# Summing the modulation's partial products: 32x32 blocks turned and added on VectorE, quarters added in column tiles on TensorE

## What is computed

```python
cond = jax.nn.silu(c)                       # (1, 2048)
mod = cond @ w_ada[l] + b_ada[l]            # (1, 6144)
shift, scale, gate = jnp.split(mod, 3, axis=-1)
h = rms_norm(x, norm_g[l]) * (1.0 + scale[:, None, :]) + shift[:, None, :]
...
x = x + gate[:, None, :] * y
```

## Time and profile before

| | |
|---|---|
| median of three runs | 2553.03 us (2550.57 to 2553.16) |
| the profiled execution, its time | 2552.88 us |
| the profiled execution, its span | 2551.6 us |
| TensorE busy | 2510.9 us, 98% of the span |
| VectorE busy | 1644.1 us, 64% |
| ScalarE busy | 842.1 us, 33% |
| GpSimd busy | 392.3 us, 15% |

### The profile page before, as it was taken

The page is one execution under the profiler, slowest core; times in us unless marked ns, Lnnn a source line. Parts: engine busy times, 40 slices in busy tenths (PEclk is TensorE's granted clock), DMA queues, the critical chain, the costliest instruction groups (busy, mean ns, idle before and its releaser), DMA issues.

```text
span 2551.6 us, 30016 instructions
## 1 busy us (share of the span) xinstructions
PE 2510.9 (98%) x11928; PEld 2175.2 (85%) x11928; DVE 1644.1 (64%) x2187; ACT 842.1 (33%) x1139; POOL 392.3 (15%) x295
## 2 busy tenths in 40 slices
PE   8989999999999999999999999989999999999997
PEld 7878888888888888888888888878888888888886
DVE  6788889888988776545455775557565563244434
ACT  5222222222222322233322333332566564333321
POOL 0035344353443421000000000020000000000001
PEclk9999999999999999999999999989999999999998
DMA  5333333333333433667666675533322222322333
GB/s 184 106 99 128 115 114 105 124 117 109 125 109 126 141 122 130 221 215 255 196 204 204 217 240 202 200 102 132 100 87 77 85 88 87 116 99 93 122 124 116
DMA packets 119867, 353.07 MB, mean 138 GB/s; under 512 B 15408, under 2 KB 22832, under 8 KB 119728
## 3 DMA queue, kind: packets, MB, share of 16 engines
q1 hardware_dynamic: 119728, 351.16, 41.4%
HBM read 321.68 MB, written 23.07 MB: 135 GB/s over the span
## 4 chain that ended last, share of the span: by engine, by line
PE 95%; DVE 2%; issue 1%; POOL 0%; ACT 0%; DMA 0%; SPq 0%; DVEq 0%; POOLq 0%; ACTq 0%
PE bank L524 28%; PE bank L525 28%; PE bank L526 28%; PE bank L691 2%; PE bank L692 2%; PE bank L693 2%; PE bank L734 1%; PE bank L724 1%; PE bank L589 1%; PE bank L577 1%; DVE X L1836 0%; DVE SO L1434 0%; PE bank L715 0%; PE bank L717 0%; PE bank L514 0%
## 5 line engine op out<-in xcount | busy, mean ns | idle before, releaser
L1153 DVE TENSOR_TENSOR WL<-W,WH 128x1024 fp32r<-128x1024 f32 (+1 forms) x456 | 602.4, 1324 | 464.5 <-ACT WH L829 463.9
L829 ACT ACTIVATE WH<-W 128x1024 fp32r<-128x1024 f32 (+1 forms) x456 | 478.2, 1051 | 940.4 <-PE bank L526 706.7
L524 PE MATMUL bank<-hH,WH 128*128 128x512 f32 x1792 | 682.7, 381 | 12.7 <-DVE WL L1153 8.6
L525 PE MATMUL bank<-hL,WH 128*128 128x512 f32 x1792 | 680.9, 380 | 0.0
L526 PE MATMUL bank<-hH,WL 128*128 128x512 f32 x1792 | 680.6, 380 | 0.0
L524 PEld LDWEIGHTS bank<-hH,WH 128*128 128x128 f32 x1792 | 339.6, 189 | 69.7 <-DVE WL L1153 9.0
L526 PEld LDWEIGHTS bank<-hH,WL 128*128 128x128 f32 x1792 | 339.7, 190 | 48.5
L525 PEld LDWEIGHTS bank<-hL,WH 128*128 128x128 f32 x1792 | 339.7, 190 | 47.9
L524 PE MATMUL bank<-h2H,WH 128*128 128x512 f32 x640 | 245.5, 384 | 0.1
L525 PE MATMUL bank<-h2L,WH 128*128 128x512 f32 x640 | 242.6, 379 | 0.0
L526 PE MATMUL bank<-h2H,WL 128*128 128x512 f32 x640 | 242.6, 379 | 0.0
(11 more groups left out here) (260 smaller groups left out, 3585.4 us busy)
## 6 DMA issues: line engine op xcount, KB each, us to landing
W<-in_w SPq DMA_DIRECT2D x335, 512.0 KB, 3.7
W<-in_ada SPq DMA_DIRECT2D x96, 512.0 KB, 4.3
W<-in_wa SPq DMA_DIRECT2D x32, 512.0 KB, 4.1
W<-in_wo SPq DMA_DIRECT2D x32, 512.0 KB, 3.8
W<-in_wvv SPq DMA_DIRECT2D x32, 512.0 KB, 3.7
W<-in_wb SPq DMA_DIRECT2D x16, 512.0 KB, 3.7
URAW<-U SPq DMA_DIRECT2D x96, 64.0 KB, 3.1
scr_am<-SO SPq DMA_DIRECT2D x16, 256.0 KB, 2.0
```

The source lines that it names most:

```text
L524: e.matmul(o, wh, xh, start=first, stop=False)
L525: e.matmul(o, wh, xl, start=False, stop=False)
L829: e.activation(WH[:, n % NB, c], W[:, i % NW, c], ACT.Copy).then_inc(sem["hi"], 1)
L1153: e.tensor_tensor(WL[:, s, c], W[:, plan.item_of[n] % NW, c], WH[:, s, c].bitcast(F32), ALU.subtract).then_inc(sem["lo_v"], 1)
```

## The change

TensorE no longer takes the sum over all 128 partitions. VectorE turns `ACC` in 32x32 blocks (`transpose`, one instruction over 128x1024) into a scratch `AT`, which lies in `T` for parts 0 to 3 and in `U` for parts 4 and 5, and adds each group of 32 neighbours (`tensor_reduce`) into `AR`, 128x32. After that only four numbers, one from each quarter of the partitions, are left to add for an output. TensorE adds them in four matmuls whose stationary operand is `SEL`, 128x32, built once from the identity; each writes its own 32 partitions of bank 3, eight columns wide. VectorE does its two steps three units ahead of the reduction (`n + 3 in plan.reduce_at`), before that unit's `lo`. The next part's first chunk waits for the turn (`ada_t`) and no longer for `MOD`.

```diff
@@ pe_program, unit
-                e.wait_ge(*nth("ada_v", cb))
+                e.wait_ge(*nth("ada_r", cb))
                 if cb > 0:
                     e.wait_ge(*nth("mod", cb - 1))
                 else:
                     e.wait_ge(*nth("skip", 7))
-                for q in range(8):
-                    mm = e.matmul(bank[3][:, q:q + 1], ACC[:, 128 * q:128 * q + 128], ONE[:, 0:1],
-                                  start=True, stop=True)
+                parts = AR[:, :].rearrange("p (q g) -> p g q", g=4)
+                for g in range(4):
+                    mm = e.matmul(bank[3][32 * g:32 * g + 32, 0:8], SEL[:, :], parts[:, g, :], start=True, stop=True,
+                                  skip_group_check=True)
                 mm.then_inc(sem["ada_pe"], 1)
@@ dve_program, ada_chunk
             if i % 16 == 0:
                 if i > 0:
-                    e.wait_ge(*nth("mod", i // 16 - 1))
+                    e.wait_ge(*nth("ada_t", i // 16 - 1))
@@ dve_program
+        def ada_sums(cb):
+            turned = AT[cb // 4]
+            if cb == 0:
+                e.tensor_reduce(SEL[:, :], IDT[:, :].rearrange("p (r a) -> p a r", r=4), AX,
+                                ALU.add).then_inc(sem["sel"], 1)
+                e.wait_ge(*nth("skip", 7))
+            if cb == 4:
+                e.wait_ge(*nth("g_v", 7))
+            e.wait_ge(*nth("ada_v", cb))
+            e.transpose(turned, ACC[:, :]).then_inc(sem["ada_t"], 1)
+            e.wait_ge(*nth("ada_t", cb))
+            if cb > 0:
+                e.wait_ge(*nth("ada_pe", cb - 1))
+            e.tensor_reduce(AR[:, :], turned.rearrange("p (c b) -> p c b", b=32), AX,
+                            ALU.add).then_inc(sem["ada_r"], 1)
+
         def unit():
             n = at_unit[0]
             at_unit[0] += 1
+            if n + 3 in plan.reduce_at:
+                ada_sums(plan.reduce_at[n + 3])
             if n in plan.reduce_at:
                 cb = plan.reduce_at[n]
                 e.wait_ge(*nth("ada_pe", cb))
```

More of the change, by code:

```diff
@@ L49 @@
     "ssm_bu": 1, "ssm_out": 1, "skip": 1,
-    "sp_v": 1, "sp_a": 1, "ada_v": 16, "ada_pe": 1, "mod": 1, "rss": 1,
+    "sp_v": 1, "sp_a": 1, "sel": 1, "ada_v": 16, "ada_t": 1, "ada_r": 1, "ada_pe": 1, "mod": 1, "rss": 1,
     "a_v": 8, "a_a": 2, "a_p": 1, "al_a": 1, "al_v": 1, "yb_a": 1, "yb_v": 1, "ma": 1, "g_a": 2, "g_v": 3, "b_v": 3, "b_a": 1,
@@ L225, in program @@
     SC = at("SC", 205, [128, 16])
+    SEL = at("SEL", 196, [128, 32])
+    AR = at("AR", 196.125, [128, 32])
+    AT = [T[:, 2:4, :].rearrange("p a b -> p (a b)"), U[:, 0:2, :].rearrange("p a b -> p (a b)")]
     ST = at("ST", 205.25, [128, 80])
```

## The result

The changed kernel takes 2542.6 us, the median of six runs (2541.67 to 2547.16). The kernel before, run six times in all, takes 2550.95 us (2550.50 to 2553.16). By the medians that is 8.4 us less. The ratio is 0.9968, with a 95% interval of 0.9957 to 0.9979; by it the kernel takes 8.2 us less, somewhere between 5.4 and 11.

A forecast was written before the change was run, and what follows sets the result against it. TensorE's row of matmuls was taken to bound the kernel. Six reductions give back 7.4 us and one stop costs 1.0, so 2552.88 - 6.4 = 2546.5 us, with a range from 2542.8 to 2550.4.

The forecast's parts named there:

- The bound: Whole kernel: TensorE, busy for 98% of the span, sets the time; a microsecond less at a reduction is one less at the end.
- The removed cost: At each of six reductions, TensorE's old sum over partitions costs 1.78 us, 10.7 us for all six.
- The price of the narrow group: TensorE's four new matmuls at each reduction: 0.55 us, with bounds of 0.35 and 1.18.
- What the 0.33 is: In each new TensorE group, 0.33 us is the price of going into the narrow shape and back.
- VectorE's two steps: VectorE, three units ahead of each reduction: turn 1.25 us, pair 2.5 us with the wait; `SEL` adds some 0.29 once.
- The cover at five places: At all reductions but the fourth, VectorE's pair costs nothing: slack is 7.8 us, 5.4 at the fifth.
- The stop at the fourth: Fourth reduction: VectorE's pair delays the last group of `BL`, so TensorE stops once for 1.0 us, bounds 0.4 or 2.2.
- cheap rounds and a short stop: Rival, chance 0.20: second-round weights in beforehand, turn 0.62 us, stop 0.4 us; 8.2 us less, 2544.7 us.
- The base: Starting time of the forecast: the profiled execution of the kernel before, 2552.88 us, 0.15 under the median.
- The range: For the whole kernel's time: 2542.8 us (the cheap case, less the spread of single runs) to 2550.4 us.
- the cheap case: Rival, chance 0.20, with cheap TensorE rounds and a short stop at the fourth reduction: 2544.7 us.

The follow-up runs named there:

- e3: Changed kernel with TensorE's four narrow matmuls only, from an `AR` zeroed once, without VectorE's turn and sum: 2541.72 us.
- e6: Changed kernel with one full 128x128 matmul (`SEL` four times side by side) in place of the four narrow ones: 2542.88 us.
- e8: Changed kernel with `ACC` turned three times over at the five reductions other than the fourth: 2543.33 us.
- e1: The changed kernel run again, unedited: 2542.71 us.
- e10: Changed kernel with the `zb` loads for stage `wg` issued one projection earlier, into four buffers in place of two: 2542.89 us.
- e5: The kernel before run again, unedited, in one execution for a second profile: 2550.72 us.
- e9: Changed kernel with one full-width matmul for the four narrow ones and the modulation begun two units later: 2542.05 us.
- e7: Changed kernel with the whole modulation begun one gate projection (two units) later: 2543.26 us.
- e4: Changed kernel with VectorE's turn and sum ahead of the fourth reduction moved one unit later: 2543.46 us.
- e2: Changed kernel with VectorE's turn and sum kept but unused, TensorE summing in eight matmuls as in the kernel before: 2552.08 us.
- e11: Changed kernel with one full-width matmul, the modulation begun two units later and the early `zb` loads together: 2540.42 us.

## Why the prediction was wrong

**The bound: right.** TensorE's row sets the time, and what is cut out of it at the six places comes off the end; e3 gives 8.47 us for six gaps of 1.40.

**The removed cost: right.** The 8.47 us of e3 are 1.41 for each reduction, which is 1.78 less the 0.38 that replaced it.

**The price of the narrow group: mis-sized.** "I take 0.11 a round: 0.33 + 0.22 = 0.55 us." It measured 0.38, near the best bound of 0.35. The sum was 0.33 and some 0.05 for the two rounds, which start 0.05 us apart, and not 0.22: the second round's weights are in before the first is done, as the read-out's eight loads in 0.16 us had shown; I took the length of one group for each round instead. That is 6 x 0.17 = 1.0 us of the miss.

**What the 0.33 is: wrong.** I called it the price of going into the narrow shape and back. e6 changes no shape, and its two records, 0.03 us apart, cost 0.23. So some 0.20 is paid by this short float32 group between full ones in the full shape too, and only 0.13 to 0.15 goes with the narrow one. The number held because it was read from rows of the same shape.

The Trainium skill's sentence "Mode switching requires drain" (TensorEngine Tiling (Array Packing), Key Properties) agrees with the measurement: the group starts 0.31 us behind the matmul ahead of it, and in e6, without a change of mode, 0.22. That is 0.09 us of the 0.38. For so little work the four column tiles cost more than one full matmul, 0.38 against 0.23.

**VectorE's two steps: right.** 1.25 was taken for the turn and 1.24 measured, 1.22 for the sum and 1.22 measured; `SEL` took 0.37 and not 0.29. `tensor_reduce` did no harm at five places; at the fourth it is half of the delay that brings the stop.

**The cover at five places: right,** by e8 with twice the work.

**The stop at the fourth: right in its place and mechanism, its size 0.6 for 1.0.** In three profiles of the pair at this place (e1, e6, e10) the gap is 0.71, which costs 0.58 of the stretch (664.28 - 663.70). The first profile shows 2.0. Of the 0.4 that 0.58 lies under the forecast, near 0.2 is in the two steps (2.40 us from start to start and not 2.5, and they begin a little before the `BL` ahead of them has ended). Some 0.13 is a late load of `SI` in the profile of before itself, at 1429.01, which was reckoned as if it belonged to the kernel; the rest is rounding. I had not reckoned that VectorE, without slack in `wg`, also hands on whatever a late load of `SI` costs it, which makes the stop an uncertain number and not a sum.

**The rivals.** The second one, cheap rounds and a short stop, was right in its rounds (0.38 a reduction) and wrong in its turn: 1.24 us and not 0.62.

**The base: the step that failed most.** "The profiled execution took 2552.88 us, 0.15 under the median, so 2552.88 - 6.4 = 2546.5 us." Three runs gave that median. Six gave 2550.95, 1.9 us less, and later groups 2551.4 to 2551.6. The profile of before started late (279.87 us to the first read-out, where e5 had 277.67). A change of 8 us in 2550 was thus forecast from a base uncertain by 2. The miss of 3.9 us is 1.9 of base, 1.0 of narrow group, 0.4 of stop, and 0.6 that the stretch doesn't explain: the medians say 8.4 and 8.7 us less, the stretch of e1 7.9. A part of that rest goes with TensorE's clock, which the forecast left out (last section); it isn't settled.

The range failed for the same reason: its lower end took the cheap case from the profiled execution. It was also added up wrong. The cheap case less 2.3 us is 2544.7 - 2.3 = 2542.4, where 2542.8 was written, and 2542.6 would have lain inside; that would have been luck, by a base 1.9 us too high and a turn at half its time.

## What to carry to other kernels

A small piece of work on the engine that sets the time is priced by the gap that it opens between its neighbours, and so is what replaces it: a short group paid 0.23 us here even in the usual shape and 0.38 in narrow tiles side by side, so one matmul of the usual shape was cheaper for the same sum. What is moved to an engine with 35% idle time is free only where that idle time lies: look at the steps queued behind it in that very stage, and at whether the engine's period there leaves anything to catch up with. When the expected change is a few thousandths, take the base from several runs and compare one stretch that holds the change, not the ends of the trace. Before a leftover wait is given a cause, look for a second profile that has the cause and not the wait, as e9 was for e7.

## What the runs showed of the hardware

A 32x32 turn of 128x1024 float32 by VectorE takes 1.24 us, near the 1.22 and 1.28 of its float32 passes with two tensor operands of that size (L1157, L1172); a pass with one, L1165 of the kernel before, takes 0.75. A narrow group of eight records with eight moving columns costs TensorE 0.38 us between full ones, at all six places; two full records with 32 columns cost 0.23, and sixteen full ones with one column, 0.106 us each on the average, 1.78.

TensorE's clock falls from 2.4 to 1.2 GHz in the pause after `wo`, where it does the short sums over tokens and waits for VectorE, and rises again in the projection that follows. In the profile of before the granted clock is 1.00 until 1686, 0.94 in 1686:1690 and 0.50 in the rows below. Where the fall and the rise come differs from run to run. The windows of before begin 2 us behind its first sum over tokens (1688.03), those of e1 3 us behind its own (1678.68); 12 us of each are shown (columns: stretch, length, busy and count for PE, PEld, DVE, ACT and POOL, granted clock, DMA share, GB/s):

```profile
1690.00:1694.00 4.00, 1.96 (x10) 1.87 (x9) 2.35 (x15) 0.41 (x2) 0.00 (x0) 0.50 0.00 0
1694.00:1698.00 4.00, 3.61 (x16) 3.48 (x16) 1.11 (x3) 0.60 (x1) 0.83 (x1) 0.50 0.00 0
1698.00:1702.00 4.00, 1.41 (x4) 1.09 (x4) 3.13 (x4) 1.38 (x3) 2.71 (x3) 0.50 0.00 0
```

```profile
1682.00:1686.00 4.00, 1.53 (x7) 1.54 (x8) 1.76 (x11) 0.20 (x1) 0.00 (x0) 0.50 0.00 0
1686.00:1690.00 4.00, 2.24 (x11) 1.95 (x10) 1.95 (x2) 1.50 (x3) 2.75 (x2) 0.73 0.00 0
1690.00:1694.00 4.00, 3.16 (x9) 2.64 (x10) 3.21 (x5) 2.39 (x4) 1.84 (x2) 0.70 0.00 0
```

In e1 the clock was back at full for part of the pause, which ends with the first matmul of the projection at 1690.84. From the first sum over tokens to the attention's first turn it is 152.15 us in both profiles of before and in e4, 152.14 in the changed kernel's first, 151.3 in e1, e2, e3, e6, e7, e8, e10 and e11, and 152.5 in e9. From that turn to the end it is 711.4 to 711.5 us in before, e5, e4 and the changed kernel's first, and 711.0 in all others. So a time moves by up to 1.3 us with it, and the same code can show either: the changed kernel was on both sides, and e2, whose work on TensorE is that of before, on the short one.

It need not fall evenly on the kernels, though. The timed executions have a mean granted clock as well. Of the 33 of the kernel before that stand beside the experiments, 23 have 0.991 or less, and their median is 2551.75 us; the other ten, at 0.992 to 0.994, have 2550.90. Of the changed kernel's eleven (with e1), ten have 0.993. So some of the difference of the medians may be the clock and not the six reductions: at 0.993 and more, before has only three executions, 2550.63 to 2550.83, and the changed kernel's ten have a median of 2542.49, 8.2 us less, where the first group gave 8.4, the second 8.7 and the stretch 7.9. Why the clock differs between the kernels isn't shown.
